# Raw rows transposed first, scales applied on the way out of PSUM, the sample's rows projected second, keys sorted ahead, and a changed end, in a one-core hybrid decoder step

## The reference, cut to what matters

```
z = rmsnorm(x) @ w_in                 # 1816 columns: pool u, q, k (3 branches), memory q, v, gates
q, k, qm = head-wise rmsnorm, rotary on the first 16 dims of q and k
mem_kv = rmsnorm(mem) @ w_mem_kv      # 256 memory rows, 512 columns
o = pooling mixer | native sparse attention (compressed, selected, window) | memory attention
h = x + concat(rmsnorm(o parts)) @ w_out
y = h + HierMoE(rmsnorm(h))           # top-1 of 4 groups, top-2 of 8 experts, 32 experts of 1024x512
```

## Time and profile before

| | |
|---|---|
| runs | 1063.87, 1068.31, 1070.82 us (median 1068.31) |
| profiled execution | 1065.07 us, span 1063.1 us, so 1.97 us lie around the span |
| busy share of the span | PE 85%, weight loads 46%, DVE 30%, ACT 18%, POOL 11% |
| moved by DMA | 273.14 MB |
| stages, us from the span's start | project to about 160, stream to 323, attention and mixer to about 580, experts to 1054, end 1063.1 |

### The profile page before, as it was taken

One profiled execution on the slowest core, in us unless ns is written; L12 is line 12 of the kernel. 1 busy time (PEld: TensorE's weight loads), 2 busy tenths in 40 slices (PEclk: granted clock), 3 DMA queues, 4 the chain that ended last, 5 costly groups with the idle time before them and its releaser, 6 DMA issues.

```text
span 1063.1 us, 13517 instructions
## 1 busy us (share of the span) xinstructions
PE 903.8 (85%) x5419; PEld 493.8 (46%) x5419; DVE 321.4 (30%) x689; ACT 195.3 (18%) x470; POOL 112.8 (11%) x131
## 2 busy tenths in 40 slices
PE   4899969999996786889998999979877787788784
PEld 2455535555565553445554555535443444344441
DVE  3333242223244568863634111101111111111110
ACT  1111122111124467561100000100000000000000
POOL 0000104121100000000000111111110110110111
PEclk9999997999999788989998999999999999999998
DMA  9754016495607000004939899999999999999992
GB/s 388 327 163 140 15 48 157 102 220 120 186 2 283 5 1 1 1 1 199 347 122 414 336 413 415 413 415 413 412 421 415 410 417 409 409 419 414 412 417 75
DMA packets 66055, 273.14 MB, mean 257 GB/s; under 512 B 11760, under 2 KB 27951, under 8 KB 40575
## 3 DMA queue, kind: packets, MB, share of 16 engines
q1 hardware_dynamic: 52215, 255.22, 61.5%
q0 software_dynamic: 7376, 12.85, 4.4%
q10 hardware_dynamic: 6400, 4.20, 1.8%
HBM read 265.68 MB, written 19.10 MB: 268 GB/s over the span
## 4 chain that ended last, share of the span: by engine, by line
PE 24%; DMA 23%; SPq 12%; DVE 6%; ACT 3%; issue 1%; POOL 0%; DVEq 0%; POOLq 0%; ACTq 0%
DMA room<-in_w_up 11%; SPq L2022 8%; PE ps L2160 6%; PE ps L1732 5%; SPq L2026 3%; PE ps L2187 3%; DMA w_b<-in_w_up 3%; DMA w_a<-in_w_gate 3%; DMA w_b<-in_w_gate 3%; DMA room<-in_w_gate 3%; DVE room L1437 2%; ACT w_a L1572 2%; PE ps L1283 1%; PE ps L1265 1%; DMA xg<-hn_dram,pairs 1%
## 5 line engine op out<-in xcount | busy, mean ns | idle before, releaser
L2160 PE MATMUL ps<-room 128*64 128x256 f32 x800 | 96.9, 389 | 32.9 <-DMA room<-in_w_up 20.3
L2160 PEld LDWEIGHTS ps<-room 128*64 128x64 f32 x800 | 55.8, 138 | 70.4 <-DMA room<-in_w_up 29.8
L2160 PE MATMUL ps<-w_a,room 128*64 128x256 f32 x576 | 69.6, 391 | 17.3 <-DMA w_a<-in_w_up 9.5
L2160 PE MATMUL ps<-w_b,room 128*64 128x256 f32 x576 | 67.8, 383 | 18.0 <-DMA w_b<-in_w_up 9.6
L445 PE MATMUL ps<-w_b,room 128*128 128x454 f32 (+1 forms) x240 | 80.9, 548 | 0.7 <-ACT room L418 0.7
L2076 POOL DMA_INDIRECT out_y<-room,halves x32 | 50.1, 1565 | 286.6 <-ACT room L2340 286.6
L2340 ACT ACTIVATE room<-ps,slot_w 128x512 f32<-128x512 f32 x32 | 22.0, 687 | 280.8 <-PE ps L2187 280.8
L897 PE MATMUL ps<-room,w_a 128*128 128x378 f32 x192 | 62.5, 483 | 0.0
L2160 PEld LDWEIGHTS ps<-w_a,room 128*64 128x64 f32 x576 | 41.1, 140 | 43.3 <-DMA w_a<-in_w_up 14.0
L2160 PEld LDWEIGHTS ps<-w_b,room 128*64 128x64 f32 x576 | 40.2, 137 | 42.9 <-DMA w_b<-in_w_up 14.6
L2251 DVE SCALAR_TENSOR_TENSOR room<-room,ps 128x256 f32<-128x256 f32 x32 | 13.5, 421 | 153.1 <-ACT room L2334 153.1
(11 more groups left out here) (358 smaller groups left out, 1193.6 us busy)
## 6 DMA issues: line engine op xcount, KB each, us to landing
room<-in_w_down SPq DMA_DIRECT2D x26, 1024.0 KB, 28.6
room<-in_w_gate SPq DMA_DIRECT2D x25, 1024.0 KB, 28.4
room<-in_w_up SPq DMA_DIRECT2D x25, 1024.0 KB, 28.3
w_a<-in_w_gate SPq DMA_DIRECT2D x18, 1024.0 KB, 27.6
w_a<-in_w_up SPq DMA_DIRECT2D x18, 1024.0 KB, 28.3
w_a<-in_w_down SPq DMA_DIRECT2D x18, 1024.0 KB, 28.0
w_b<-in_w_gate SPq DMA_DIRECT2D x18, 1024.0 KB, 27.6
w_b<-in_w_up SPq DMA_DIRECT2D x18, 1024.0 KB, 28.3
```

The costliest lines, as they stand in the source:

```text
L2160: ins = nc.tensor.matmul(ps[h * CAP:h * CAP + CAP, bank, 0:FH], xT[:, n // 2 % 2, k, CAP * slot:CAP * slot + CAP], w[k // 4][:, k % 4, h * ...
```

## The change

1. `project`: rows are transposed raw as soon as they and the identity (now a load of its own, first among the constants) are in. `take_x` moves to DVE and multiplies by the gains, which lie along the partitions then (`g_cols`, 2 x 8 columns, loaded from ACT's queue in runs of 8 floats; `g_rows` is not loaded). The row factor is applied by ACT as the scale of the copy out of PSUM (`keep`). The sample's rows are scaled on ACT before their transposes (`row_scaled`). x has a buffer for each item, `w_mem` comes in two halves, the other constants after `w_in`.
2. The sample is item 3, after the first tile, in PSUM banks 6 and 7. The last tile's heads are done in two parts: 17 heads when three of four chunks are out, one head after the fourth.
3. On DVE `take_x(t + 1)` stands before `norm(t + 2)` and `heads(t)`; on ACT `root(t + 2)` stands after the squares of t.
4. `stream`: POOL sorts the keys of the first two halves early, their values later; ACT issues the first window and memory key loads before its last copies of `project`; the NB half waits for the prompt's key and value stores alone (`kv_stored`).
5. `experts`: the last four units load in the order 93, 94, 92, 95, the order of their use. The last wait for scatters stands behind `needed`; the block ends with `no_gpsimd_drain=True`, and the last `close` has no barrier.

The diff, cut:

```diff
-    def close(self, stage):
+    def close(self, stage, last=False):
         stage.close()
         self.nc.clear_and_free_semaphores(self.stage_sems)
-        self.nc.all_engine_barrier()
+        if not last:
+            self.nc.all_engine_barrier()
...
-        first, sample = 2, 2 + TILES
+        first, sample = 2, 3
+        rows = [P, P, P, NB] + [P] * (TILES - 1)
+        tile_of = [None, None, 0, TILES] + list(range(1, TILES))
+        slot = [0, 1, 0, None, 1, 0, 1]
+        early_heads = (3 * ZC - Q0) // HD
...
+            load_x(0)
+            sp.dma_start(self.consts[:, C_ID:C_ID + P], I["consts"][:, C_ID:C_ID + P]).then_inc(ident_in, 16)
+            for j in range(2):
+                sp.dma_start(w_mem[:, 4 * j:4 * j + 4, :], ...).then_inc(wmem_in[j], 16)
+                load_x(j + 1)
             for j in range(4):
-                sp.dma_start(early[:, 2 * j:2 * j + 2, :] ...).then_inc(win_in, 16)
+                sp.dma_start(early[:, 2 * j:2 * j + 2, :] ...).then_inc(win_in[j], 16)
                 if j == 0:
                     sp.dma_start(g_head[:, :], ...).then_inc(head_in, 16)
+                    load_x(sample)
+                if j == 2:
+                    load_x(4)
+            sp.dma_start(self.consts[:, C_CAUS:CW], ...).then_inc(consts_in, 16)
+            load_x(5)
+            load_x(6)
...
+            sp.wait_ge(xT_in_psum, sample + 1)
             for i in range(2):
                 self.load_half(sp, i)
...
+            def take_x(t):
+                if t == 0:
+                    dve.wait_ge(gains_in, 16)
+                dve.wait_ge(xT_in_psum, t + 1)
+                if t != sample and slot[t] in slot[:t]:
+                    dve.wait_ge(z_in_psum, ...)
+                nc.vector.tensor_tensor(turned_rows(t)[:, :, 0:r], pt[:, :, 0:r], g_cols[...].broadcast_to([P, KD, r]), ALU.mult).then_inc(xT_ready, 1)
...
+            take_x(0)
             norm(0)
             norm(1)
             for t in range(n_items):
+                if t + 1 < n_items:
+                    take_x(t + 1)
                 if t + 2 < n_items:
                     norm(t + 2)
-                heads(t)
+                if t < n_items - 1:
+                    heads(t, 0, groups(t)[1], t)
+            heads(n_items - 1, 0, early_heads, n_items - 1)
+            heads(n_items - 1, early_heads, NG, n_items)
...
+            act.dma_start(g_cols[:, :, :], I["g_rows"].rearrange("j (p k) -> p j k", k=KD)).then_inc(gains_in, 16)
+            def keep(t, a):
+                act.wait_ge(z_in_psum, done(t) + a + 1)
+                    nc.scalar.activation(dst, in_psum(t, a), ACT.Copy, scale=stat[0:rows[t], t, 3:4]).then_inc(z_ready, 1)
...
 # TensorE
-                pe.wait_ge(xn_ready, t + 1)
+                if t != sample:
+                    pe.wait_ge(x_in[t], 16)
+                else:
+                    pe.wait_ge(row_scaled, 1)
                 if t >= 1:
                     pe.wait_ge(xT_ready, t)
...
-            pe.wait_ge(consts_in, 16)
+            pe.wait_ge(ident_in, 16)
             turn(0)
             for t in range(n_items):
-                if t + 1 < n_items:
+                if first < t < n_items - 1:
                     turn(t + 1)
# turn(1) and turn(2) now stand after k = 3 of the memory products, turn(3) after k = 5 of item 2
...
 # stream
-            dve.wait_ge(self.heads_done, N_ITEMS)
+            dve.wait_ge(self.heads_done, self.heads_all)
...
-                    sp.wait_ge(self.stored, 16 * (2 + 4 * TILES + 5 + 1))
+                    sp.wait_ge(self.kv_stored, 16 * 2 * TILES)
...
+            pool.wait_ge(self.turned_x, 2)
+            pool.wait_ge(self.norm_done, 2)
+            for i in range(2):
+                self.half_in(pool, i)
+                take_kv(i)
...
 # experts
-        with self.nc.Block("attend_to_experts") as block:
+        with self.nc.Block("attend_to_experts", no_gpsimd_drain=True) as block:
-        self.close(st_e)
+        self.close(st_e, last=True)
-            again += [u for u in range(RING, NU) if u not in again]
+            again += [u for u in range(RING, NU - 4) if u not in again]
+            again += [NU - 3, NU - 2, NU - 4, NU - 1]
...
             pool.wait_ge(self.moved, 32)
-            pool.wait_ge(y_out, 16 * NEXP)
             with needed(pool):
+                pool.wait_ge(y_out, 16 * NEXP)
...
+            pool.wait_ge(y_out, 16 * NEXP)
```

More of the change, by code:

```diff
@@ L259, in project @@
         self.z_chunks = sum(chunks)
+        self.heads_all = N_ITEMS + 1
         done = lambda t: sum(chunks[:t])
@@ new lines, in squares, with roots @@
+            def squares(t, lo, hi, part):
+                r, at = rows[t], groups(t)[0]
+                if t >= 2 and lo == 0:
+                    act.wait_ge(z_done, t - 1)
+                nc.scalar.activation(junk[0:r, t % 2, lo * HD:hi * HD], zt(t)[0:r, at + lo * HD:at + hi * HD], ACT.Square).then_inc(sq_ready, 1)
+            def roots(t, lo, hi, part):
+                act.wait_ge(gms_ready, part + 1)
+                nc.scalar.activation(gstat[0:rows[t], t, lo:hi], gstat[0:rows[t], t, lo:hi], ACT.Sqrt).then_inc(grms_ready, 1)
@@ L406, in scalar @@
             root(0)
             root(1)
-            take_x(0)
-            for t in range(n_items):
-                r = rows[t]
-                if t + 1 < n_items:
-                    take_x(t + 1)
+            for t in range(n_items - 1):
+                act.wait_ge(rstd_ready, t + 1)
+                for a in range(chunks[t]):
+                    keep(t, a)
+                act.wait_ge(z_ready, done(t + 1))
+                n = groups(t)[1]
+                squares(t, 0, n, t)
                 if t + 2 < n_items:
@@ L424, in scalar @@
-                roots(t)
+                roots(t, 0, n, t)
+                if t + 2 == sample:
+                    act.wait_ge(rstd_ready, sample + 1)
+                    x = xin[sample][0:NB, :]
+                    nc.scalar.activation(x, x, ACT.Copy, scale=stat[0:NB, sample, 3:4]).then_inc(row_scaled, 1)
+            t = n_items - 1
+            act.wait_ge(rstd_ready, n_items)
+            act.wait_ge(xT_in_psum, n_items)
+            for b in range(2):
+                self.load_new_keys(act, b)
@@ L426, in tensor @@
+            for a in range(3):
+                keep(t, a)
+            act.wait_ge(z_ready, done(t) + 3)
+            squares(t, 0, early_heads, t)
+            roots(t, 0, early_heads, t)
+            keep(t, 3)
+            act.wait_ge(z_ready, done(t) + 4)
+            squares(t, early_heads, NG, n_items)
+            roots(t, early_heads, NG, n_items)
         def tensor(pe):
             def turn(t):
-                r = rows[t]
-                pe.wait_ge(xn_ready, t + 1)
+                r, x = rows[t], xin[t]
+                if t != sample:
+                    pe.wait_ge(x_in[t], 16)
+                else:
+                    pe.wait_ge(row_scaled, 1)
@@ L438, in bank_free @@
                     pe.wait_ge(z_ready, a + 1)
-                if t > first:
-                    pe.wait_ge(z_ready, done(t - 1) + a + 1)
+                if t > sample:
+                    pe.wait_ge(z_ready, done(first if t == sample + 1 else t - 1) + a + 1)
             def product(t, a, k):
```

208 lines of the change are left out of this document (102 added, 106 removed).

## The result

Before: 1067.97 us (median of 4 runs, 1063.87 to 1070.82). After: 1034.48 us (4 runs, 1032.72 to 1036.87). The ratio is 0.9691, 95% interval 0.9653 to 0.9728: 33.5 us faster. Measured again later beside other kernels, the changed kernel had 1037.71 us (6 runs, 1034.16 to 1039.87) against 1064.33 of the kernel before, ratio 0.9745 (0.9713 to 0.9776), 26.6 us. The forecast, 1037.0, lies between the two; as a ratio it was 0.9707. The profiled executions, 1065.07 and 1036.87 us, differ by 28.2.

What follows compares the result with a forecast made beforehand. Experts were taken as bound by their weight stream (414 GB/s), which starts when earlier stages let it. Gains of 18.0 + 4 + 8.8 = 30.8 from the 1068.3 median gave 1037.5, forecast as 1037, range 1029 to 1050.

Steps and rivals of the forecast that it cites:

- The start: Start of `project`: first prompt tile starts on PE at 27.0 us instead of 41.48, a gain of 14.5 us.
- Rival (a): Start of `project`: gains land late and hold up PE; 1048 us (chance 0.13), or 1065 behind all SP loads (0.03).
- The order of the items: `project` with the sample after the first tile: PE ends it at 136.9 us, against 149.8.
- The added wait: Before tile 1 in `project`: PE stands still 2.9 us for `take_x(4)`, queued behind `heads(2)` on DVE.
- From project to stream: Last tile's heads end sooner, so PE's third turn in `stream` comes at 140.2 us instead of 158.20: 18.0 gained.
- The clock in stream: Early `stream`: PE's shorter pause leaves the clock full, a gain of 4 us, with 0 as the other end.
- Between: Rest of the kernel up to 1000 us, after early `stream`: shifts unchanged by 22 us.
- Rival (c): `stream`: slow confirmation of the last tile's stores delays the NB half, up to 10 us lost, 1047 us; chance 0.06.
- the prediction's own signs: Profile after: experts' weight stream 22 us earlier, PEclk 1.0 at `stream`'s third turn, weight rate not below 414 GB/s.
- The end: End of `experts`: load order gains 3.2 us, earlier count read 1.3, no drain 4.05, no barrier 0.3; sum 8.8.
- rival (b): Clock stays half into `stream`, or drain moves behind the span: 4 us less each, 1041, both 1045; chance 0.14.
- parts 1 to 3: Forecast steps for the start of `project`, the order of its items, and the passage to `stream`; together 18.0 us gained.

Runs made afterwards that it cites:

- the tail alone: Kernel before with only the end's edits (order of last loads, no drain, no last barrier, earlier scatter wait): 1056.11 us against 1065.26, ratio 0.9917.
- the filled pause: Changed kernel with 20 repeated transposes behind the second unit of `stream`, before PE's pause: 1039.55 us (one run).
- the take sooner: Changed kernel with `take_x(4)`, for tile 1, put ahead of tile 0's heads on DVE: 1035.12 us (6 runs), ratio to before 0.9726.
- the keys sorted late: Changed kernel with the first two halves' keys copied behind the memsets and the new keys' half loaded behind all stores: 1042.58 us (one run).
- the gains late: Changed kernel with the gains' load on SP's queue behind all input weights, not on ACT's at the start: 1066.05 us (one run).

## Why the prediction was right, point by point

**The start**, 14.5 us forecast, 13.1 measured (tile 0 at 28.36, not 27.0). Turn 0 was sooner than I put it (4.62, not 5.2), the gains were hidden (4.3 us, not 5.0), and `take_x` took the 1.22 of the earlier trace rows. Product 0 was mis-sized: its first eight matmuls took 6.27 us, the later eight 3.60, so that it took 9.9 and not 8.44, and it began at 8.97 by the landing of `w_mem`, which I hadn't costed. I had put the slow first part of this product down to a half clock; no row shows that, as the granted clock is at 1.00 up to 36 us in both traces, and why these matmuls take longer stays open. The row factor isn't quite free either: ACT's copy out took 0.69 us for 0.58 over 512 columns (0.64 for 0.54 over 454), and PE waits 1.04 us for one of them ahead of tile 0. Rival (a) didn't come. Its price was right: behind the whole of SP's loads I had put 1065, and that kernel measured 1066.05. Of the Trainium skill, DMA: Bandwidth & Descriptors, the section Queues, rings and completion order (an engine takes packets from its queues in turn) agrees with what was measured, 3.6 us to landing on a queue of its own and 26.6 behind the weights; but the first load was also issued at 0.73 us, before the traffic was full (DMA share 0.68 in the first 5 us), and no run has it on ACT's queue later. The small runs of 32 bytes, on which its section Specifications would have been slow, didn't show at 8 KB.

**The order of the items**: project's end on PE at 136.9 forecast, 138.76 measured; 1.4 of the 1.9 us are the start's. The added wait was foreseen in its place and nearly its size (2.9 forecast, 2.50 measured). What failed in this step is that I priced it as itself alone: in five of six traces with the wait, though not in the one set against this forecast, the half clock behind it adds 1.7 us. Nor did I ask what the move is worth without the split: 1.2 us, by these runs, and less than nothing with the wait that it brings.

**From project to stream**: third turn at 140.2 forecast, 142.52 measured, 2.3 late with 1.9 of it inherited. The rest, 0.4, is less than the 0.7 us that DVE's rotations took longer beside POOL's copies (1.53 for 0.83); the 8.2 us of the earlier trace rows had no such neighbour. To put the sort of the values there as free was the slip.

**The clock in stream**: a gain of 4 forecast; from the third turn to the first compress the changed kernel took 20.8 us and the one before 24.8, so 4.0. By other traces of the two it is 22.6 (the tail alone, which has the old stream) and 19.8 (the changed kernel again), so the gain lies between 1.8 and 5.0, and the exact 4.0 is luck. The reason was wrong: "the clock stays full" doesn't hold (0.58 in one slice here, full in the second trace), and it doesn't hang on the pause's length, as the filled pause shows.

**Between**: "shifts unchanged by 22 us" came out as 19.7 at the first compress and 18.5 at the first gate. Rival (c) didn't come: the NB half was asked for at 145.25, and the last compress moved by 19.9, as the first did. So two of the prediction's own signs failed: the experts start 18.5 us sooner and not 22, and the clock wasn't at 1.0 behind the third turn. Of the missing 3.5 us, 2.3 were gone by the third turn; the other 1.2 lie between the last compress and the first gate, which I had put as unchanged and where executions of one kernel differ by more than that (last section). The weights' rate held, 412 to 415 GB/s in each 100 us from 600 to 1000.

**The end**: 3.2 + 5.6 = 8.8 forecast. Measured 4.4 + 5.7 = 10.1 at the checkpoints of the tail alone, 9.2 by its times, and 4.0 + 5.7 = 9.7 in the changed kernel; down 30 still waited 0.72 us for its weights. Of rival (b), the drain didn't move to behind the span: 2.0 us lie around it, as before.

Sum of the profiled pair: 18.0 + 4 + 8.8 = 30.8 forecast, 15.7 + 4.0 - 1.2 + 9.7 = 28.2 measured (third turn, clock, between, end). By the medians of the first comparison 33.5, of the second 26.6. So the 1037.0 was right by its own steps, with errors of parts 1 to 3 (2.3), of the middle (1.2) and of the end (-0.9) partly against each other. That the median came out below the forecast although the pair fell short of it is luck of the executions: the profiled one lay 2.9 under its median before and 2.4 above it after. Where the gain comes from, by the second set of medians: the tail 9, the start and the turns of raw rows 16, the move and the split together 1, as long as the wait is in; 4 without it. The last two differences lie within overlapping intervals; the traces, from tile 0 to the first compress, put them at 3 to 4 and at 5 to 6.

## What to carry to other kernels

Cost a new wait on the engine that sets the pace with what follows it: in this kernel waits of 2.5 and 5 us cost up to 4.2 us at the fourth turn and 10.5 us at the first compress. When an item is moved ahead, look first at what the other engines have queued in front of the operation it needs, and move that too. Read small edits at checkpoints of the trace, counted from the last one that both kernels share, and not at the end.

## What was not expected of the hardware

The stages between the last compress and the first gate are the same in all kernels with the new `project`, and took 280.7 to 288.0 us in twelve traces. The ends of the range are two executions of one kernel, the one with the take sooner; windows of the first and of the second:

```profile
285.00:365.00 80.00, 63.00 (x679) 44.72 (x680) 38.26 (x80) 34.14 (x122) 0.29 (x1) 0.85 0.27 96
365.00:445.00 80.00, 64.22 (x372) 34.91 (x373) 63.88 (x143) 52.30 (x147) 4.40 (x3) 0.89 0.00 1
```

```profile
285.00:365.00 80.00, 65.66 (x663) 44.94 (x663) 36.01 (x77) 34.08 (x120) 0.29 (x1) 0.77 0.26 96
365.00:445.00 80.00, 66.34 (x346) 34.46 (x345) 61.93 (x135) 48.55 (x136) 4.40 (x3) 0.82 0.00 1
```

PE's clock was granted at 0.85 and 0.89 in one and at 0.77 and 0.82 in the other, and 7.3 us arise here; the second had been 0.7 us ahead at the last compress, and ended 5.0 later (1037.8 against 1032.8). What set the clock apart in the two isn't known.

POOL's copies held up single operations of DVE: the four rotations, 0.83 us elsewhere, took 1.1 to 1.7 where the copies ran beside most of them, in the kernel before too (1.25 at 149.58). In the run with the keys sorted late an operation of 0.18 us, which began inside the four copies shown above (93.80 to 96.07), ended as they did:

```profile
94.34 1.76 DVE L388 TENSOR_SCALAR w_b<-w_b 128x18 f32<-128x18 f32 x1
```

Such meetings also made the wait of 3.68 us with the gains late (0.53 for 0.18 and 1.67 for 0.83). So a copy moved to POOL's idle time is free only if DVE's chain that is on the path doesn't run beside it.

Further, the heads of 8 rows cost DVE as much as those of 128: one multiplication over 1152 columns took 1.34 us for the sample and 1.36 for a tile.
